# Half-swap by one round of DMAs, index weighing moved up, and both LRU gates of a head in one product of 64 rows

## What is computed

```python
for l in range(DEPTH):                                  # DEPTH = 2
    h = x * (1.0 + sc1) + sh1
    p = h @ w_in[l]
    q, k, v, qi, ki, wi, xr, yg = jnp.split(p, split_at, axis=-1)
    qi = apply_rope(qi.reshape(B, S, IDX_HEADS, IDX_HEAD_DIM), cos_i, sin_i)   # 8 heads of 64
    ki = apply_rope(ki[:, :, None, :], cos_i, sin_i)[:, :, 0, :]
    attn_out = dsa_attention(q, k, v, qi, ki, wi)
    xc = causal_depthwise_conv(xr, conv_w[l], conv_b[l])
    lru_out = rg_lru(xc, w_gate_a[l], b_gate_a[l], w_gate_x[l], b_gate_x[l], lru_lambda[l])
    lru_out = lru_out * jax.nn.gelu(yg, approximate=True)
    ...                                                 # norms, output projection, MLP

# apply_rope: y = concat([x1*cos - x2*sin, x2*cos + x1*sin]), x1 and x2 the two halves of a head
# dsa_attention, per query block: top 128 causal keys by
rel = jax.nn.relu(jnp.einsum('bthd,bsd->bths', qi_b, ki32))
idx_score = jnp.einsum('bths,bth->bts', rel, wi_b)
# rg_lru: 8 blocks of 64 channels
r = jax.nn.sigmoid(jnp.einsum('bsnc,ncd->bsnd', xb, w_a).reshape(B, S, -1) + b_a)
i = jax.nn.sigmoid(jnp.einsum('bsnc,ncd->bsnd', xb, w_x).reshape(B, S, -1) + b_x)
log_a = -LRU_C * r * jax.nn.softplus(-lam)
a = jnp.exp(log_a)
u = jnp.sqrt(-jnp.expm1(2.0 * log_a)) * (i * xf)        # then the scan h = a*h + u
```

## Time and profile before

| | us |
|---|---|
| median of three runs | 1291.38 |
| lowest and highest of them | 1291.08 and 1292.97 |
| the profiled execution, whole time | 1294.84 |
| its span (first to last instruction) | 1293.1 |

### The profile page before, as it was taken

One profiled execution on the slowest core, in us unless ns is written; L12 is line 12 of the kernel. 1 busy time (PEld: TensorE's weight loads), 2 busy tenths in 40 slices (PEclk: granted clock), 3 DMA queues, 4 the chain that ended last, 5 costly groups with the idle time before them and its releaser, 6 DMA issues.

```text
span 1293.1 us, 16839 instructions
## 1 busy us (share of the span) xinstructions
PE 1255.4 (97%) x6036; PEld 994.1 (77%) x6036; DVE 832.9 (64%) x1387; ACT 541.8 (42%) x818; POOL 159.6 (12%) x127
## 2 busy tenths in 40 slices
PE   7999999999999999999999999989999999999996
PEld 5765767787888888888877666778778888888885
DVE  4478995756875765768767999585654353443354
ACT  4643458536513313314245535863462241331331
POOL 0100345110000000001110014501100000000012
PEclk9989999999999999999999999999999999999998
DMA  9953544331554563656224222202133333333321
GB/s 316 308 173 128 164 130 163 115 98 33 183 178 144 172 216 100 226 163 215 84 77 122 75 80 66 81 18 82 34 119 98 94 96 97 97 97 98 98 66 66
DMA packets 78774, 160.66 MB, mean 124 GB/s; under 512 B 6784, under 2 KB 17272, under 8 KB 78712
## 3 DMA queue, kind: packets, MB, share of 16 engines
q1 hardware_dynamic: 66176, 114.90, 28.7%
q0 software_dynamic: 11136, 42.47, 9.8%
q10 hardware_dynamic: 1400, 2.49, 0.8%
HBM read 155.64 MB, written 2.10 MB: 122 GB/s over the span
## 4 chain that ended last, share of the span: by engine, by line
PE 78%; DVE 8%; ACT 6%; issue 3%; DMA 3%; SPq 2%; ACTq 0%; POOL 0%; POOLq 0%; DVEq 0%
PE bank L702 24%; PE bank L704 23%; PE bank L703 23%; PE bank L909 1%; DMA w_raw<-in_w_in_dram 1%; DVE idx_acc L1767 1%; DMA x_in<-in_x_dram 1%; DVE idx_acc L1785 1%; PE bank L583 1%; DMA turned_ring<-xc 1%; PE bank L749 1%; DVE w_lo L1576 1%; ACT a_hi L1082 1%; DVE best L1783 1%; ACT turned_ring L1166 1%
## 5 line engine op out<-in xcount | busy, mean ns | idle before, releaser
L1071 ACT ACTIVATE w_hi<-w_raw 128x1024 fp32r<-128x1024 f32 x192 | 201.9, 1057 | 460.9 <-PE bank L704 451.2
L1576 DVE TENSOR_TENSOR w_lo<-w_raw,w_hi 128x1024 fp32r<-128x1024 f32 x168 | 206.3, 1234 | 252.9 <-ACT w_hi L1071 252.5
L702 PE MATMUL bank<-a_hi,w_hi 128*128 128x512 f32 x896 | 360.1, 402 | 8.0 <-ACT turned_ring L1248 2.9
L704 PE MATMUL bank<-a_hi,w_lo 128*128 128x512 f32 x896 | 350.1, 391 | 0.0
L703 PE MATMUL bank<-a_lo,w_hi 128*128 128x512 f32 x896 | 349.6, 390 | 0.0
L702 PEld LDWEIGHTS bank<-a_hi,w_hi 128*128 128x128 f32 x896 | 168.6, 188 | 67.6 <-issue 26.3
L702 PE MATMUL bank<-b_hi,w_hi 128*128 128x512 f32 x512 | 199.7, 390 | 0.0
L704 PE MATMUL bank<-b_hi,w_lo 128*128 128x512 f32 x512 | 199.3, 389 | 0.0
L703 PE MATMUL bank<-b_lo,w_hi 128*128 128x512 f32 x512 | 199.2, 389 | 0.0
L704 PEld LDWEIGHTS bank<-a_hi,w_lo 128*128 128x128 f32 x896 | 168.6, 188 | 36.2
L703 PEld LDWEIGHTS bank<-a_lo,w_hi 128*128 128x128 f32 x896 | 168.8, 188 | 34.8 <-issue 1.9
(11 more groups left out here) (265 smaller groups left out, 1401.9 us busy)
## 6 DMA issues: line engine op xcount, KB each, us to landing
mod_raw<-in_w_mod_dram POOLq DMA_DIRECT2D x40, 1024.0 KB, 5.9
w_raw<-in_w_up_dram SPq DMA_DIRECT2D x64, 512.0 KB, 3.7
w_raw<-in_w_down_dram SPq DMA_DIRECT2D x64, 512.0 KB, 3.8
w_raw<-in_w_in_dram SPq DMA_DIRECT2D x48, 512.0 KB, 3.7
first_mod<-in_w_mod_dram SPq DMA_DIRECT2D x8, 1024.0 KB, 12.2
w_raw<-in_w_out_dram SPq DMA_DIRECT2D x16, 512.0 KB, 3.7
x_in<-in_x_dram SPq DMA_DIRECT2D x4, 512.0 KB, 11.7
turned_ring<-xc ACTq DMA_DIRECT2D x16, 128.0 KB, 7.0
```

The costliest lines, as they stand in the source:

```text
L702: mm(o, wh, hi(kk), start=first, stop=False)
L704: last = mm(o, wl, hi(kk), start=False, stop=fin)
L1071: last = af(hi, src, ACT.Copy)
L1576: last = tt(lo, src, hi.bitcast(F32), ALU.subtract)
```

## The change

**Swap.** The eight DMAs of the half-swap become four. Each moves 32 partitions of all four tiles (32x2048) after all four qi copies, and there is one semaphore for all of them, on which every `qi_sine(m)` and `xr_out` wait. The copies of the ki bank (`kiwi_copies`) move up, right behind the four DMAs and ahead of the last weight pair of xr.

**Weighing.** The four pairs of query tile 1 go from positions 14, 17, 19, 21 to 14, 17, 20, 23. On DVE, the first two heads of query tile 1 are added before xr's last low part, and the rest alternates with the low parts of v. `topk(18)` leaves its place ahead of k's third low part; its rounds are spread over the places behind it, now (19, 24, 29, 34) instead of (22, 26, 30, 34).

**Gates.** `gate_blocks` now holds both gates side by side: for the first block of a tile (rows 0 to 63) the columns of r, then of i; for the second block (rows 64 to 127) those of i, then of r. One product of 64 rows by 128 columns per block gives both gates of the block. So `gate_pair(m)` is two matmuls of 64 rows, block 0 into bank 4 and block 1 into bank 5, and both banks must be free ahead of the first. In each bank one half is r in its own partitions, the other half is i in the partitions of the other block. `gate_out(m)` is now four sigmoids of 64 partitions; i goes into a new tile `gi_swapped` (lru_gate_swapped, in the memory of yg's result). After each second m, ACT waits for its own sigmoids and issues two DMAs of 64x1024 that exchange the halves into `gi`. `gated`, and `yg_out` for the memory, wait for them. POOL's memset of the block-diagonal matrix goes, and two small copies by DVE (`bx`, the exchanged bias) come in `layer_vectors`.

```diff
-                        pool.dma_start(blk[64 * par:64 * par + 64, g, :, 64 * par:64 * par + 64],
+                        at = 64 * (g ^ par)
+                        pool.dma_start(blk[64 * par:64 * par + 64, :, at:at + 64],
...
-                    pool.wait_ge(free_s[5], uses_before(5, f"gi{m}", l) + 1)
+                    pool.wait_ge(gates_swapped[m // 2], 32 * (l + 1))
...
                         if (name, p) == lows[5]:
-                            for m in range(LT - 1):
-                                gated(m)
+                            gated(0)
+                            gated(1)
                         if (name, p) == lows[7]:
-                            gated(LT - 1)
+                            gated(2)
+                            gated(3)
...
-                    **dict(zip((14, 17, 19, 21), (idx_pair(1, j) for j in range(IDX_HEADS // 2)))),
+                    **dict(zip((14, 17, 20, 23), (idx_pair(1, j) for j in range(IDX_HEADS // 2)))),
...
-                        for g, (b, name) in enumerate(((4, f"gr{m}"), (5, f"gi{m}"))):
-                            pe.wait_ge(free_s[b], uses_before(b, name, l))
-                            mm(banks[b][:, :], blk[:, g, m, :], xc[:, m, :], start=True, stop=True).then_inc(full_s[b], 1)
+                        pe.wait_ge(free_s[4], uses_before(4, f"gr{m}", l))
+                        pe.wait_ge(free_s[5], uses_before(5, f"gi{m}", l))
+                        for b, rows in ((4, slice(0, 64)), (5, slice(64, P))):
+                            mm(banks[b][:, :], blk[rows, m, :], xc[rows, m, :], start=True, stop=True).then_inc(full_s[b], 1)
...
-                def swap_qi(j):
+                def swap_qi():
...
-                    for m in (2 * j, 2 * j + 1):
+                    for m in range(4):
                         act.wait_ge(free_s[m], uses_before(m, f"qi{m}", l) + 1)
...
-                        act.dma_start(ring[at:at + half, 2 * j:2 * j + 2, :], xc[src:src + half, 2 * j:2 * j + 2, :])\
-                            .then_inc(qi_swapped[j], 16)
+                        act.dma_start(ring[at:at + half, :, :], xc[src:src + half, :, :]).then_inc(qi_swapped, 16)
...
-                        if m % 2:
-                            swap_qi(m // 2)
+                    swap_qi()
+                    kiwi_copies()
...
+                    for j in range(2):
+                        act.wait_ge(gates_swapped[j], 32 * (l + 1))
                     for m in range(LT):
                         act.wait_ge(full_s[m], uses_before(m, f"yg{m}", l) + 1)
...
-                    for b, name, dst, bias in ((4, "gr", th, "b_gate_a"), (5, "gi", gi, "b_gate_x")):
-                        act.wait_ge(full_s[b], uses_before(b, f"{name}{m}", l) + 1)
-                        af(dst[:, m, :], banks[b][:, :], ACT.Sigmoid, bias=vcol(bias, m)).then_inc(free_s[b], 1)
+                    for b, name, r, i in ((4, f"gr{m}", slice(0, 64), slice(64, P)), (5, f"gi{m}", slice(64, P), slice(0, 64))):
+                        act.wait_ge(full_s[b], uses_before(b, name, l) + 1)
+                        af(th[r, m, :], banks[b][r, :], ACT.Sigmoid, bias=vec[r, at:at + 1])
+                        af(gi_swapped[i, m, :], banks[b][i, :], ACT.Sigmoid, bias=bx[i, m:m + 1]).then_inc(free_s[b], 1)
+                    if m % 2:
+                        pair = slice(m - 1, m + 1)
+                        act.wait_ge(free_s[4], uses_before(4, f"gr{m}", l) + 1)
+                        act.wait_ge(free_s[5], uses_before(5, f"gi{m}", l) + 1)
+                        act.dma_start(gi[0:64, pair, :], gi_swapped[64:P, pair, :]).then_inc(gates_swapped[m // 2], 16)
+                        act.dma_start(gi[64:P, pair, :], gi_swapped[0:64, pair, :]).then_inc(gates_swapped[m // 2], 16)
...
-                slot(l, "xr", (none, qi_cosines, qi_sines))
+                split_lo("xr", l, 0)
+                split_lo("xr", l, 1)
+                qi_cosines()
+                split_lo("xr", l, 2)
+                qi_sines()
...
+                idx_add(1, range(0, 2))
+                split_lo("xr", l, PAIRS - 1)
+                idx_add(1, range(2, 4))
                 split_lo("v", l, 0)
-                idx_add(1, range(0, 2))
-                idx_add(1, range(2, 4))
+                idx_add(1, range(4, 6))
                 split_lo("v", l, 1)
-                idx_add(1, range(4, 6))
                 idx_add(1, range(6, 8))
...
-                topk(18)
                 split_lo("k", l, 2)
...
-                for p, rounds_ in enumerate((22, 26, 30, 34)):
+                for p, rounds_ in enumerate((19, 24, 29, 34)):
```

More of the change, by code:

```diff
@@ L297, in trunk_kernel @@
         gate_in = sem("gate_in")
+        gates_swapped = [sem(f"gates_swapped{j}") for j in range(2)]
         xn_ready = sem("xn_ready")
@@ L303, in trunk_kernel @@
         ff_sq = sem("ff_squared")
-        rope_done, qi_cos, qi_swapped = sem("rope_done"), sem("qi_by_cosine"), [sem(f"qi_swapped{j}") for j in range(2)]
+        rope_done, qi_cos, qi_swapped = sem("rope_done"), sem("qi_by_cosine"), sem("qi_halves_swapped")
         idx_acc = sem("idx_accumulated")
@@ L475, in _ @@
             gp.memset(ones_d[:, :], 1.0 / D).then_inc(p_const, 1)
[L476 removed]
             gp.memset(eps[:, :], LN_EPS).then_inc(p_const, 1)
[L478 removed]
+            pool.wait_ge(p_const, 6)
             def layer(l):
@@ L1175, in swap_qi, with kiwi_copies @@
                         src = at + half if at % IDX_DH == 0 else at - half
-                        act.dma_start(ring[at:at + half, 2 * j:2 * j + 2, :], xc[src:src + half, 2 * j:2 * j + 2, :])\
-                            .then_inc(qi_swapped[j], 16)
+                        act.dma_start(ring[at:at + half, :, :], xc[src:src + half, :, :]).then_inc(qi_swapped, 16)
+                def kiwi_copies():
+                    act.wait_ge(full_s[4], uses_before(4, "kiwi", l) + 1)
+                    if l == 0:
+                        act.wait_ge(p_sin, 7)
+                    af(kiwi[0:KIWI, :], banks[4][0:KIWI, :], ACT.Copy)
+                    af(kiwi_swapped[0:32, :], banks[4][32:64, :], ACT.Copy)
+                    af(kiwi_swapped[32:64, :], banks[4][0:32, :], ACT.Copy).then_inc(free_s[4], 1)
                 def qi_out():
@@ L1182, in qi_out @@
                         af(xc[:, m, :], banks[m][:, :], ACT.Copy).then_inc(free_s[m], 1)
[L1183 to L1184 removed]
+                    swap_qi()
+                    kiwi_copies()
                 act.wait_ge(vec_ready, l + 1)
                 slot(l, "xr", qi_out)
[L1188 to L1193 removed]
                 def xr_out():
                     act.wait_ge(qi_cos, l * 4 + 4)
[L1197 to L1198 removed]
+                    act.wait_ge(qi_swapped, 64 * (l + 1))
                     for m in range(LT):
```

25 lines of the change are left out of this document (11 added, 14 removed).

## The result

| | us |
|---|---|
| before, median of 4 runs | 1292.18 |
| after, median of 4 runs (1304.04 to 1307.93) | 1307.03 |
| after over before, ratio with its 95% interval | 1.0106 (1.0092 to 1.0120) |
| the profiled execution of after, and its span | 1306.48 and 1304.8 |

The change makes the kernel 13.7 us slower by the ratio (11.9 to 15.5). The forecast was 1299.4, 8.0 slower. The sign was right, and the time lies on the upper end of the range of 1290 to 1307, above the 1295 to 1304 that the forecast gave its own case.

A forecast was written before the change was run, and what follows sets the result against it. PE, busy 97% of the span, was taken as the bound. Swap and weighing -4.0, start of k -0.6, layer 1 net -0.7, gates +5.0, clock +8.3: +8.0 on 1291.4 gives 1299.4 us, range 1290 to 1307.

The forecast's parts named there:

- That 64 partitions cost ACT what 128 do: Gates on ACT: half the partitions cost the same, so a gate's two sigmoids of together 1.2 us become four of 2.4.
- The wait of 2.5 ahead of gate 1: In q, both layers: PE waits 2.5 us instead of 0.56 for both banks, a net loss of 0.9.
- The waits one by one at yg's banks: Start of yg: PE waits three times (layer 0) or four times (layer 1) about 1.15 us between single positions.
- the delay of yg's fourth bank: Start of yg: the fourth bank starts 2.5 us later in each layer, +5.0, containing the loss at gate 1.
- The wait at position 10 of v: Layer 1: PE's wait of 0.45 us becomes 1.85, +1.4, as query tile 1's pair 3 stands two positions later.
- The start of k in both layers: With topk(18) moved, PE's wait of 0.6 us goes in layer 0; in layer 1 about 0.2 remains of 2.27, -2.1.
- The price of a product pair of 64 rows: Gates on PE: a pair costs 1.25 us against 1.71, saving 0.46 in each of eight pairs.
- Crediting half of the spell: Layer 0's low-clock spell costs 3.3 us in the profile; whether timed runs have it is open, so 1.65 is credited.
- the landing of the one round: xr of layer 0: the last transfer lands near 70, PE's pair at position 14 waits for nothing, gain 4.0 us.
- the second rival: The half-swap lands late, PE waits at position 14, the 4.0 isn't gained: 1303.4 to 1304.7 us, chance 0.25.
- equal packet counts: Swap queue's 131 packets beside q0's 128: a queue with larger packets gets more bytes, favouring the early landing.
- the clock: Low clock after new waits: 3.3 us for one fall at gate 1, 2.5 at yg in each layer, together +8.3.

The follow-up runs named there:

- wide_sp: wide_gates with all three exchange transfers per two gates issued by SP and POOL's gated products back where the change has them: 1294.43 us, ratio 1.0005.
- no_gates: The changed kernel with the gates of the kernel before (one swap round, weighing moved up, topk(18) spread): 1295.22 us, ratio 1.0010.
- small_rows: no_gates with the one round of the half-swap cut into eight DMAs of 32x1024, rows of 4 KB: 1295.47 us, one run.
- hold_one_round: no_gates with the 1 MB load of late modulation weights held until the half-swap's one round has landed: 1291.52 us, ratio 0.9984.
- gates_only: The kernel before with the change's gates alone; half-swap, weighing and topk as before: 1302.62 us, ratio 1.0078.
- narrow_sp: gates_only with the four exchange DMAs of a layer issued by SP in place of ACT: 1300.88 us, ratio 1.0062.
- gates_spread: gates_only with the gate products at positions 6, 15, 19, 24 of q in place of 6, 12, 18, 24: 1296.95 us, ratio 1.0032.
- wide_gates: The kernel before with the change's 64-row products, two sigmoids of 128 partitions per gate, and all exchange transfers issued by POOL: 1307.88 us, ratio 1.0099.
- hold: The kernel before with POOL's 1 MB load of late modulation weights in layer 0 held until both half-swap rounds have landed: 1291.60 us, ratio 0.9983.
- hold_moved: two_rounds with the 1 MB load held until the half-swap has landed, and query tile 1's pairs moved in layer 0 alone: 1287.74 us, ratio 0.9959.
- two_rounds: no_gates with the two-round half-swap of the kernel before: 1290.96 us, ratio 0.9977.

## Why the prediction came out as it did

**Right, by its own steps.** That 64 partitions cost ACT what 128 do: a sigmoid of 64x512 takes 0.67 to 0.69 in after, one of 128x512 took 0.69. The wait of 2.5 ahead of gate 1, in both layers. The waits one by one at yg's banks and the delay of yg's fourth bank (5.0 forecast; 2.9 + 3.0 = 5.9 measured without the clock). The wait at position 10 of v (1.85 forecast, 1.81 measured). The start of k in both layers. The price of a product pair of 64 rows, 1.25: around gate 3 of after it is 182.05 - 180.34 - 2 x 0.23 = 1.25. And 1.5 us are saved from q to yg where ACT holds it up less (wide_sp), of the 1.8 that four times 0.46 would be.

```profile
180.34 0.39 PE L708 MATMUL bank<-a_hi,w_lo 128*128 128x512 f32 x1
...
182.05 0.39 PE L707 MATMUL bank<-a_lo,w_hi 128*128 128x512 f32 x1
```

Crediting half of the spell of the kernel before was sound too: its 25 runs beside the last group go from 1290.40 at a mean clock of 0.996 to 1295.19 at 0.993, as if some had it and some not.

**Wrong: the landing of the one round.** The step said: "If one large round moves like that, the last lands near 70", and took this end over 72.5 to 74.6. It landed at 73.9, the second rival's case: issue to landing was 8.6 to 13.7, where the step carried over the 7.0 to 10.4 of transfers of half the size. The row I leaned on, equal packet counts, was read rightly (159 beside 164 and 168), but I left out what hangs on it. A packet of twice the bytes also holds the engine more than twice as long, 73 against 64 us of engine time a MB in no_gates and small_rows, so the turn gets longer for all. That the other queues are what the transfer is late by is shown by hold_one_round, 70.3 without the one load; that the longer turn eats up the larger packet is read from the counts, and small_rows, with both rows in one mix, lands at the same time. The later issue is not the miss: it was in the working, at 1.1, and was 0.7. The engines have work of other queues already then; the queues of the kernel before in 57 to 61 us, with the first four swap DMAs issued from 57.46, show nothing of q10:

```profile
q0 software_dynamic: 187, 0.77, 50.5%
q1 hardware_dynamic: 246, 0.47, 47.1%
```

The second rival had this case at 0.25 with 1303.4 to 1304.7. One sum in it is off: a landing at 74.6 makes PE wait 4.6 at position 14 and not 3.6, since after's pair starts 1.5 behind the landing, and 71.43 is where it is due. After's landing at 73.9 gave 4.04. In the ledger the step is a miss of 4.3, the largest of the rows, in a sum that fell short by 3.6.

**Mis-sized: the clock.** I gave the gates 8.3. In the trace of after they cost 3.4, two spells of 1.7 behind the two waits of 2.5, and nothing at yg; gates_only and narrow_sp have one at yg in layer 1, gates_spread in both layers. I had priced a fall at 3.3 from the one in the earlier trace rows, which is a spell of double length; of thirteen more traces only wide_gates has another such. And the same two waits had none behind them in gates_only, and the timed runs of gates_only differ by about three spells, so the 3.4 is that of one execution. In exchange two spells came where I had none, at position 10 of v and in the attention. So the sum over all places is 5 x 1.7 = 8.5 in after against 3.4 before. What decides whether a wait has a spell behind it stays open.

**Left out: the attention of layer 1.** A wait of 1.51 became 1.95 with a spell, 1.9 in all. I had looked for slack behind q_out and found none, which was right, but not at what DVE and POOL would then do side by side. That this is the cause is read from the rows of the fourteen traces and not shown by a run; by far the larger part, 1.7, is the spell.

## What to carry to other kernels

Before two transfers are merged into one, ask which part of the data is wanted first and what else is on the DMA engines at that time; holding back one load that is not due for 20 us was worth 2.2 us here, the reordering on DVE 3.0. An operation on half the partitions saved nothing on ScalarE here (0.68 beside 0.69), so a product that delivers its results split over partition halves doubles the work behind it; if it is done, take the bank out whole. Count the waits of PE that a change moves and not only those that it removes, since each may cost a spell at the low clock, up to 1.7 us beside the wait. And compare the mean clock of the profiled run with that of the timed ones before a ledger from one trace is taken for the median.

## What the runs showed of the hardware

- A tensor-by-tensor product on DVE with both inputs in SBUF stood still through two POOL products, two DMA issues of POOL and a third product: 6.78 us in place of 0.69. MAX8 and MATCH_REPLACE8 beside POOL's products of the same kind (the kernel before, 176.43 to 180.20) kept their 0.68 to 0.70.
- Ahead of the last 15 us of each kernel the low clock comes in spells of one length: 1.7 us lost where PE is busy, in 28 places of fourteen traces, and twice double. Where PE waits during it, it costs less: the one at yg in layer 1 of gates_only cost 0.8. The same wait has it in one kernel and not in the next: 2.27 at the start of k without (before), 2.25 with (hold, PEclk 0.50 in 752 to 755); 2.52 at gate 1 without (gates_only), 2.55 with (after, layer 0); 2.02 in the attention without (hold_moved), 1.98 with (two_rounds).
- In SBUF-to-SBUF transfers rows of 8 KB cost 73 us of DMA engine time a MB (no_gates; 78 in after) and rows of 4 KB 64 (small_rows; 60 in the kernel before), all in 63 to 71 us in a mix with two other queues; alone with SP's loads it is 73 (hold_one_round: 79.1% of 16 engines for 5 us for 0.87 MB) and 66 (hold: 60.5% for 0.73 MB).
